# The recurrence's decay products with half as many VectorE instructions, each over both sides of every pair of blocks

## The reference

```python
xn = _rmsnorm(x, norm_pre_w[l])
h = xn @ w_in[l]                       # 2048 x 13312
na_q, na_k, na_v, na_z, hg_q, hg_ff, hg_fb, hg_i, hg_z, gate_pre = jnp.split(h, splits, axis=-1)
o_a = neighbourhood_attention(na_q, na_k, na_v, rpb) * silu(na_z)
o_b = rmsnorm(hgrn2_bidirectional(hg_q, hg_ff, hg_fb, hg_i, lb), hg_norm_w) * silu(hg_z)
g_a, g_b = split(sigmoid(gate_pre + b_gate))
y = g_a * (o_a @ w_branch[:1024]) + g_b * (o_b @ w_branch[1024:])
x = x + _rmsnorm(y @ w_out[l], norm_post_w[l])
```

```python
f = lb + (1 - lb) * sigmoid(fl);  k = (1 - lb) * sigmoid(-fl)
S_t = diag(f_t) S_{t-1} + k_t outer v_t;  o_t = S_t^T q_t
```

## Time and profile before

| | us |
|---|---|
| median of 3 runs | 861.75 (859.98 to 862.22) |
| the profiled execution | 860.45 |
| its span, first to last instruction | 858.7 |
| TensorE matmuls busy | 841.0 |
| TensorE weight loads busy | 731.2 |
| VectorE busy, 1304 instructions | 637.3 |
| ScalarE busy | 404.3 |
| GpSimd busy | 45.2 |
| mean share of the DMA queue q1 | 62.8% |
| mean granted TensorE clock | 0.996 |

### The profile page before, as it was taken

How to read it: one execution, slowest core, us unless ns; L and a number is a source line. 1 busy time by engine, 2 the same in 40 slices (tenths; PEclk the granted TensorE clock), 3 DMA queues, 4 the chain that set the end, 5 groups by cost and what they waited for, 6 DMA issues and landing times.

```text
span 858.7 us, 14528 instructions
## 1 busy us (share of the span) xinstructions
PE 841.0 (98%) x4913; PEld 731.2 (85%) x4913; DVE 637.3 (74%) x1304; ACT 404.3 (47%) x667; POOL 45.2 (5%) x51
## 2 busy tenths in 40 slices
PE   6999999999999999999999999999999999999995
PEld 6888888888888888888888888888888888888884
DVE  4767786886888788688768877886875678874444
ACT  5453444536445443543454454445444555554442
POOL 5300000100100000010000001000000000000002
PEclk9999999999999999999999999999999999999998
DMA  8967657666665665666576656657565766675522
GB/s 241 279 186 174 189 147 188 173 172 170 165 180 162 165 187 157 183 159 170 165 182 167 182 156 160 190 148 194 147 187 162 221 186 187 187 281 210 192 98 99
DMA packets 270967, 153.44 MB, mean 179 GB/s; under 512 B 15241, under 2 KB 261089, under 8 KB 270305
## 3 DMA queue, kind: packets, MB, share of 16 engines
q1 hardware_dynamic: 269936, 149.17, 62.8%
q10 hardware_dynamic: 1008, 3.98, 1.2%
HBM read 151.04 MB, written 2.10 MB: 178 GB/s over the span
## 4 chain that ended last, share of the span: by engine, by line
PE 94%; DMA 2%; SPq 1%; DVE 1%; ACT 1%; POOL 0%; DVEq 0%; issue 0%; ACTq 0%
PE psum L960 51%; PE psum L962 26%; PE psum L1034 3%; PE psum L1155 3%; PE psum L1157 3%; PE psum L1156 3%; DMA raw<-in_w_in 2%; SPq L267 1%; PE psum L1020 1%; PE psum L1009 1%; PE psum L989 1%; PE psum L1047 1%; DVE w_lo L597 0%; PE psum L1039 0%; PE psum L998 0%; PE psum L1054 0%
## 5 line engine op out<-in xcount | busy, mean ns | idle before, releaser
L960 PE MATMUL psum<-act_hl,w_hi 128*128 128x512 f32 x1664 | 593.5, 400 | 0.7 <-DVE w_lo L597 0.5
L962 PE MATMUL psum<-act_hl,w_lo 128*128 128x256 f32 x1664 | 463.9, 279 | 0.0
L597 DVE TENSOR_TENSOR w_lo<-raw,w_hi 128x1024 fp32r<-128x1024 f32 x270 | 328.4, 1256 | 76.9 <-ACT w_hi L387 76.7
L960 PEld LDWEIGHTS psum<-act_hl,w_hi 128*128 128x128 f32 x1664 | 312.3, 188 | 74.4 <-DVE w_lo L597 3.5
L962 PEld LDWEIGHTS psum<-act_hl,w_lo 128*128 128x128 f32 x1664 | 313.6, 188 | 0.0
L387 ACT ACTIVATE w_hi<-raw 128x1024 fp32r<-128x1024 f32 x272 | 272.9, 1051 | 33.4 <-PE psum L1157 25.6
L398 ACT ACTIVATE part<-psum 128x256 f32<-128x256 f32 x104 | 39.7, 382 | 257.8 <-PE psum L962 257.8
L960 PE MATMUL psum<-branch_hl,w_hi 128*128 128x512 f32 x256 | 89.0, 392 | 0.0
L962 PE MATMUL psum<-branch_hl,w_lo 128*128 128x256 f32 x256 | 71.7, 280 | 0.0
L960 PEld LDWEIGHTS psum<-branch_hl,w_hi 128*128 128x128 f32 x256 | 47.9, 187 | 10.8 <-DVE branch_hl L763 0.3
L657 DVE TENSOR_TENSOR hg<-hg 128x128 f32<-128x128 f32 x224 | 51.2, 290 | 0.3
(11 more groups left out here) (124 smaller groups left out, 543.6 us busy)
## 6 DMA issues: line engine op xcount, KB each, us to landing
raw<-in_w_in SPq DMA_DIRECT2D x104, 1024.0 KB, 5.7
raw<-in_w_branch SPq DMA_DIRECT2D x16, 1024.0 KB, 6.0
raw<-in_w_out SPq DMA_DIRECT2D x16, 1024.0 KB, 5.1
bias_t<-in_na_rel_bias SPq DMA_DIRECT2D x32, 96.0 KB, 5.7
big<-in_x SPq DMA_DIRECT2D x2, 1024.0 KB, 6.3
big<-in_x ACTq DMA_DIRECT2D x2, 1024.0 KB, 6.6
out<-big SPq DMA_DIRECT2D x5, 256.0 KB, 2.7
wide<-in_norm_post_w ACTq DMA_DIRECT2D x1, 1024.0 KB, 4.6
```

Of the source, the lines that this page charges most:

```text
L597: nc.vector.tensor_tensor(w_lo[:, i, :], raw[:, r, 1024 * h:1024 * (h + 1)], w_hi[:, i, :].bitcast(F32), ALU.subtract).then_inc(lo_ready, 1)
L960: nc.tensor.matmul(sums[h][:, :], w_hi[:, i, w], operand[:, k, :], start=first, stop=False, skip_group_check=True)
L962: ins = nc.tensor.matmul(sums[h][:, 0:T], w_lo[:, i, w], operand[:, k, 0:T], start=False, stop=last, skip_group_check=True)
```

## The change

Every pair of VectorE instructions that did the left and the right side of the pairs of blocks becomes one. A new helper, `sides`, builds an access pattern with a dimension of two between the pair and the element: its stride leads from the left block's place in one buffer to the right block's place in another. The four products are put next to each other in the order `suf_b, pre_f, suf_f, pre_b`, and `key_f, key_b` side by side, all in the same tile `hg`. `grow` has two instructions in place of four, the second waiting for the first in full; `decayed` has two in place of four. What is computed per element is unchanged, and so is the order of the parts.

```diff
-        pre_f, suf_f, suf_b, pre_b, hq, key_f, key_b, key_s, i_feat, hz, hth, o_h, o_sq, rst_rows = (
+        suf_b, pre_f, suf_f, pre_b, key_f, key_b, hq, key_s, i_feat, hz, hth, o_h, o_sq, rst_rows = (
             hg[:, i, :] for i in range(14))
...
-            na_s, hg_s, ob_s = Steps(na_step, 3), Steps(hg_step, 2 * 2 + 1 + 1 + 4 * (LEVELS - 1)), Steps(ob_step, 2)
+            na_s, hg_s, ob_s = Steps(na_step, 3), Steps(hg_step, 2 * 2 + 1 + 1 + 2 * (LEVELS - 1)), Steps(ob_step, 2)
...
+            def sides(left, right, half, left_at=0, right_at=None, spread=1):
+
+                start = left.offset + left_at
+                step = right.offset + (half if right_at is None else right_at) - start
+                return bass.AP(left.tensor, start, [list(left.ap[0]), [2 * half, T // (2 * half)], [step, 2], [spread, half]])
+
             def grow(half):
 
-                def bc(ap, side, pos):
-                    return pairs(ap, half)[:, :, side, pos:pos + 1].to_broadcast([P, T // (2 * half), half])
-                for i, (dst, side, src) in enumerate((
-                        (suf_f, 0, bc(pre_f, 1, half - 1)), (pre_b, 1, bc(suf_b, 0, 0)),
-                        (pre_f, 1, bc(pre_f, 0, half - 1)), (suf_b, 0, bc(suf_b, 1, 0)))):
-                    if i >= 2:
-                        hg_s.settle(dve, but=1)
-                    d = pairs(dst, half)[:, :, side, :]
-                    hg_s.done(nc.vector.tensor_tensor(d, d, src, ALU.mult))
+                hg_s.done(nc.vector.tensor_tensor(sides(suf_f, pre_b, half), sides(suf_f, pre_b, half),
+                                                  sides(pre_f, suf_b, half, 2 * half - 1, 0, 0), ALU.mult))
+                hg_s.settle(dve)
+                hg_s.done(nc.vector.tensor_tensor(sides(suf_b, pre_f, half), sides(suf_b, pre_f, half),
+                                                  sides(suf_b, pre_f, half, half, half - 1, 0), ALU.mult))
...
-                for dst, side, v, w in ((q_dec, 1, hq, pre_f), (q_dec, 0, hq, suf_b),
-                                        (k_dec, 0, key_f, suf_f), (k_dec, 1, key_b, pre_b)):
-                    ins = nc.vector.tensor_tensor(*(pairs(i, half)[:, :, side, :] for i in (dst[:, b, :], v, w)),
-                                                  ALU.mult)
-                ins.then_inc(dec_ready, 1)
+                q_out, k_out = q_dec[:, b, :], k_dec[:, b, :]
+                nc.vector.tensor_tensor(sides(q_out, q_out, half), sides(hq, hq, half), sides(suf_b, pre_f, half), ALU.mult)
+                nc.vector.tensor_tensor(sides(k_out, k_out, half), sides(key_f, key_b, half),
+                                        sides(suf_f, pre_b, half), ALU.mult).then_inc(dec_ready, 1)
```

More of the change, by code:

```diff
@@ L236, in column @@
             return ap[:, i:i + 1] if isinstance(i, int) else ap[:, bass.ds(i, 1)]
-        def pairs(ap, half):
-            return ap.rearrange("p (n two h) -> p n two h", two=2, h=half)
         def both_tiles(ap):
```

## The result

The changed kernel takes **865.42 us** (median; 863.38 to 867.51), the kernel before, measured beside it, 861.16 (859.98 to 862.25). The ratio is 1.0042, 95% interval 1.0032 to 1.0053: slower by 2.8 to 4.6 us, outside the range that was given. The profiled execution of the changed kernel took 863.38 us, with a span of 861.6, so 2.9 us of span are to be found beside the earlier trace rows.

What follows compares the result with a forecast made beforehand. TensorE's matmuls were taken as the bound (841.0 of 858.7 us); about 10 us saved on VectorE would go into waits, so 860.45 + 0 us profiled, 861.7 predicted as median, range 858.8 to 864.6.

Steps and rivals of the forecast that it cites:

- the range that was given: Whole kernel: 858.8 to 864.6 us, around a predicted 861.7.
- The count and the price of the instructions: VectorE's grow and decays: 240 fewer, 1304 to 1064; each new one 0.42 us, 0.33 start to start.
- the 626 of the sum: VectorE's busy time: about 10 us saved in grow and decays, 637 to about 626.
- The forms at half = 1: Grow and decays hopping between two buffers at every element: 0.42 us taken; at 0.86 the end still wouldn't move.
- Rival 1: Recurrence: slow two-buffer walk makes VectorE the bound from 0.86 us per new instruction; 880 us at 1.0; chance 0.04.
- Nothing of the saving reaches the end: Recurrence levels: products released 0.15 us earlier, but TensorE comes later anyway, 1.7 us in hand at level 1; 0 gained.
- where it was named: VectorE's waits for ScalarE's part (43.1 us) and w_hi (76.7 us): longer by up to 10 us.
- TensorE as the bound of the loop: Loop over groups: TensorE's own program sets the pace, passes 76.01 us apart, tiles 6.00 or 6.10 us.
- rivals 2 and 3: Projection tiles: 2, longer beat, 7.2 us or 2.4 slower, chance 0.04; 3, long tiles fall to 6.00, 2.4 us faster, 0.05.
- the last line of the sum: Layout, other engines: only buffers change places; TensorE's matmuls, ScalarE's copies and all DMAs unchanged, 0 us.

Runs made afterwards that it cites:

- experiment 6: The changed kernel with grow and the decays as plain 256-element multiplications of contiguous buffers, same instruction places, products wrong: 866.10 us, ratio 1.0061.
- 2: The changed kernel with 40 tiny memsets at VectorE's start, so its branch loop holds no border: 861.10 us, ratio 0.9998.
- 9: The changed kernel with VectorE's branch loop written out, the same work without a register: 861.77 us, ratio 0.9996.
- 5: The changed kernel without the back-edge hint in VectorE's branch loop: 865.65 us, ratio 1.0057.
- 4: The kernel before with 61 memsets at VectorE's start, moving its branch loop to 544 to 621: 861.99 us, ratio 1.0004.
- 7: Only grow in the new form, the decays as in the kernel before; VectorE's branch loop at 448 to 525: 864.55 us, ratio 1.0039.
- 10: The changed kernel with 20 memsets at VectorE's start, branch loop at 436 to 513: 864.02 us, ratio 1.0030.
- 1: The changed kernel run again, unaltered: 864.76 us, ratio 1.0041.
- 3: The changed kernel with 67 memsets at VectorE's start, branch loop back at 483 to 560: 861.98 us, ratio 1.0006.
- 8: Only the decays in the new form, grow as in the kernel before; branch loop at 451 to 528: 861.40 us, ratio 1.0003.
- 12: The changed kernel with the branch stage's 16 weight loads cut from 1 MB to 128 KB, all instructions in place: 861.62 us, ratio 0.9998.

## Why the prediction was wrong, point by point

- **The count and the price of the instructions: right.** 1064 instructions; 629.8 us busy, inside 622 to 634, though 3.8 above the 626 of the sum. The upper end of that range has room for dearer forms at half = 1, for which no row of the kernel before has a figure; the changed kernel's trace shows 0.21 and 0.08 us more (next point). Most new ones take what L763 takes, and 8 x 2 x (0.21 + 0.08) = 4.6 us is about that difference. The lines of grow's two and the decays' two instructions (count; ns shortest, median, longest; starts; form):

```profile
L652 DVE TENSOR_TENSOR hg<-hg x56: 415/418/1524, 77.4 to 645.6; 128x256 f32<-128x256 f32 x56
L655 DVE TENSOR_TENSOR hg<-hg x56: 424/426/636, 79.0 to 646.1; 128x256 f32<-128x256 f32 x56
L667 DVE TENSOR_TENSOR q_dec<-hg x64: 424/425/499, 70.6 to 646.5; 128x256 f32<-128x256 f32 x64
L668 DVE TENSOR_TENSOR k_dec<-hg x64: 415/418/504, 71.0 to 646.9; 128x256 f32<-128x256 f32 x64
```

- **The forms at half = 1: dearer, but not the bound.** Those that hop between two buffers at every element cost more: grow at half = 1 takes 0.63 us, 0.21 above the others, and a decay at level 0 takes 0.50, 0.08 above. Rival 1 needed four at 0.86. The price falls at 4 instructions a group and doesn't reach the end: experiment 6, without it, is no faster.
- **Nothing of the saving reaches the end: right.** With the code moved off the border (2), or the loop written out (9), the change stands at 0.9998 and 0.9996, and both intervals contain 1. The passes stay at 76.01 to 76.02 us and no wait before the score matmuls (L1032 now) is listed. VectorE's wait for ScalarE's part in the recurrence grew only from 43.1 to 44.0 us, that for w_hi fell from 76.7 to 75.1, and the other waits for part, for the tiles na and big, rose together from 37.4 to 44.2: there the released time went, not where it was named.
- **TensorE as the bound of the loop, and its pace (rivals 2 and 3): right.** The earlier trace rows has its matmuls busy 76.00 of 76.00 us in both passes at a granted clock of 1.00 and VectorE 60.35 and 60.55; that leaves the 16 us a pass with which rival 1 counts. A pair of projection matmuls starts 0.35 us after the pair ahead of it (177.51 and 177.86 before), so 16 pairs make 5.6 us of a tile, in both kernels. The tiles keep their 6.0 and 6.1 us.
- **The step that failed** is the last line of the sum, "no other engine's instruction changes in count or size. 0". It counted what instructions do and not where they stand, and so had 0 for the branch stage, without a reason. The same edit that takes 240 executions away takes 67 instructions out of the code ahead of the branch loop, and so puts position 448 into that loop's first pass; the price is 3.0 us of TensorE. No rival covered it, because each asked what the new instructions do in the stage where they run. The rows that could have raised the doubt were in the trace of the kernel before: the instruction queue's packets in the page's third part, and "ACT part L527 <- PE psum L962: 4.8, 11, 3.0" among ScalarE's waits. Ten of these eleven take 1.8 us together and one takes 3.0, the stop that ends at 711.91. The profile puts it down to TensorE there, but names it issue at the same place in other traces (2.8 us in 2, 2.9 in 9).

**What the other executions lose besides.** The medians differ by 4.3 us, more than the 3.0. Two traces show what can come on top. In 5 and 6 TensorE's granted clock was 0.50 from 715.67 us, after the idle time, and 1.00 again from 719.1 us on. Experiment 5:

```profile
714.00:716.00 2.00, 0.70 (x3) 0.66 (x4) 2.00 (x3) 0.42 (x1) 0.00 (x0) 0.92 0.01 4
716.00:718.00 2.00, 2.00 (x8) 1.71 (x7) 1.74 (x6) 1.44 (x3) 0.00 (x0) 0.50 0.14 34
```

The second row has 8 matmuls in 2 us at 0.50; the changed kernel has 13 in the same stretch, at 1.00. From 715.50 to 719.00 us the counts are 12 in 5 and 13 in 6, against 22 in the changed kernel and 21 in its repeat. Nine fewer, at 3.50 us for 21 or 22 (0.16 us each), are about 1.5 us, an estimate from these counts. The span of 5 is 863.9 us, that of the repeat, with the same stop and no fall of the clock, 862.0. The six executions of the changed kernel fit: the two fastest (863.38 and 864.35) have a mean clock of 0.997, the other four 0.993 to 0.996, the slowest (867.51) the lowest. Only two such traces were taken, and why the clock fell in them and not in the changed kernel's own, after the same 3 us of idle time, they don't show.

**What stays open.** It isn't settled how far ahead of its use a block is asked for, why a second packet sometimes follows the first at once (4) and sometimes not, and why the loop over groups shows no stop. The theory that register instructions make the packet late fits runs 4, 7, 9 and 10, but only the loop as a whole was exchanged, so it is argued and not shown. A rival stands beside it untested: with the registers the written-out loop also loses the unconditional branch that leads into the loop (number 414 in the changed kernel), and the stops of 7 and 10 come right behind that branch.

## What to carry to other kernels

A change in the number of instructions moves all code behind it on that engine. Here 67 fewer cost TensorE 3.0 us (2.1 to 3.1 in the six traces with such a stop and long loads) in a stage that the diff doesn't touch. When a local change ends a few microseconds off, look for "issue" among the waits and for a large packet of the instruction queue in the gap, and shift the code by some dozens of empty instructions before judging the idea. Whether such a stop reaches the end depends on the buffered work of the engine behind it (2.3 us was free here, 4.5 cost 2.1, 4.6 cost 2.2 and 5.3 cost 3.0) and on what transfer is under way (5.3 us with loads of 1 MB, 2.3 with 128 KB). An engine with time to spare gave nothing back here when made faster, but still cost everyone time when it stopped for longer than its buffers lasted.

## What the runs showed of the hardware that I had not expected

- VectorE stood 4.5 to 5.3 us in the middle of the kernel where the profile shows no semaphore that it waits for, in six traces (the changed kernel, 1, 5, 6, 7 and 10), each time with an 8192-byte packet of q14 begun inside the stop. With the code moved by 40 or 67 places (2, 3) the stop was gone. ScalarE stood 1.9 us in the changed kernel and 2.7 to 3.0 in 2, 3, 8, 9 and the kernel before, with its number 320 next. Plain code cost nothing at position 448 (9: 0.34 us from start to start, as elsewhere), and VectorE's waits of the kernel before list no such stop in the loop over groups.
- The instruction packet came behind data: the stop was 5.3 us with a 1 MB load under way and 2.3 with loads of 128 KB (12), and in five traces (the changed kernel, 1, 6, 7 and 10) the instruction packet began 0.03 us after the last packet of a load did.
- After about 3 us without matmuls TensorE's granted clock was 0.50 for 3.4 us in two of four traces (5, 6) and 1.00 in the other two (the changed kernel and 1).
- Forty or more added instructions can make a kernel faster (2: 861.10 us against 864.76 on the same chip).
